# Two transformer blocks on one core: the order of the wide and the narrow matmuls in the two-half weight blocks

## The chip, the cores and the metric

The kernel runs on one core of one Trainium2 chip. The metric is the device time of one execution in microseconds (us). Three runs of the kernel before stand behind the median.

## What is computed

The reference is two blocks over 256 tokens of width 2048, all in float32. The first is a sliding-window attention with a gated short convolution beside it, an output projection and a gate. The second has a recurrent branch, an attention over the 64 best keys of each token, and a layer of 16384 small experts, of which each token takes 16 for each of 8 heads. Nearly all of the work is products of 256 tokens with 2048-wide weight matrices. The part that matters most here is the expert layer:

```
xf = rmsnorm(x, g)                       # 256 tokens x 2048
z  = xf . u[e]     for every expert e    # 16384 experts, 128 blocks of 128
act = gelu(z) * gate[e]                  # the gate is 0 for experts that a token did not pick
out = sum over e of act * v[e]
```

The kernel computes z for all experts densely. It builds the gate table from the picks with small products of one-hot rows, one for each token ("gate products").

## The kernel before, in words

**Units and slots.** All weights come as one stream of 904 units of 128x1024 floats (512 KB). SyncE loads them into four slots of `raw`. Each float32 weight is split in two rounded halves: ScalarE copies `raw` into `w_hi` (`split_hi`, the ACTIVATE of L470), and VectorE subtracts it from `raw` and writes `w_lo` (`split_lo`, L479). Two units make a pair, and one pair is one block of 128 output columns over all 2048 inputs. The slots hold two pairs, so that the splits work two pairs ahead of TensorE (`ahead`).

**The semaphores of a slot.** `hi_ready` counts units copied by ScalarE, `lo_ready` units subtracted by VectorE, `unit_done` units that TensorE has finished. ScalarE may write unit k of `w_hi` when unit k-4 is done: `act.wait_ge(unit_done, 2 * pair + u - 3)`. SyncE loads a slot of `raw` again when `lo_ready` says that its unit is subtracted.

**The two-half form.** `halves_out` (L510 to L528) makes one block. For each of its 16 rows of tiles it runs a wide matmul (L519: the tile of `w_hi` against 512 columns, the high and the low half of the activations side by side) and a narrow one (L526: the tile of `w_lo` against the 256 columns of the high half). It does so unit by unit: eight wide, eight narrow, eight wide, eight narrow. `unit_done` is counted behind the narrow ones of each unit. The result lies in one PSUM bank, whose second half is then copied by ScalarE (`low_half`, L532) and whose first half is added to it by VectorE (`add_halves`, L537, which counts `summed`).

**Who calls it.** 240 blocks are made so: 32 in the convolution, 32 in the recurrent branch, 32 in the heads, 32 in the router turns, 16 in the stage `u_decode`, 64 in the stage `u_gates` and 32 in the stage `u_late`. The other products have forms of their own (`tokens_out`, `columns_out`, `expert`) and are not touched.

**The stage `u_gates`**, 64 blocks, i = 0 to 31 and n = 0, 1. TensorE waits before each block until the GELU of the block two before is done, and puts four gate products (L2307) between the wide and the narrow matmuls of the second unit:

```
L2313 for n in range(2):
L2313     pe.wait_ge(gelu_ready[n], i + (2 * PH + 1))
L2314     halves_out(..., banks[2 + n], between=lambda: four_tokens(i, n))
```

ScalarE's order in one turn is written out in `gates_turn` (L1077 to L1090):

```
ahead(split_hi, act, "u_gates", i, 2, n, units=(0,))    # first unit, two pairs ahead
save_gelu(i, n - 1)                                     # GELU of the block before (L1072), its DMA (L1074)
(two copies out of the banks of the gate products, L1084)
ahead(split_hi, act, "u_gates", i, 2, n, units=(1,))    # second unit
low_half(act, GZ[:, n, :], banks[2 + n])                # L532
```

VectorE's order in one turn (L1854 to L1861) is: `split_lo` of the first unit, four `weighted` tiles for the next gate products (`four_tiles`, L1848), `split_lo` of the second unit, `add_halves`, and two additions out of the banks of the gate products (L1842). GpSimd makes the four `hot` tiles (L663).

**The stage `u_decode`** has ScalarE's order `split_hi` of the first unit, GELU of the block before (L1049) with its DMA (L1051), `low_half`, `split_hi` of the second unit; VectorE puts large pieces of the router's decoding between its splits (`next_low`). TensorE waits there for `summed` of the block two before. In the other stages, but for the recurrent branch, ScalarE splits both units of a pair one behind the other. In the first router block TensorE waits ahead of the second unit's wide matmuls for the low halves of the activations (`fills`, L513), which VectorE is then still writing (L1199).

Of the kernel before, what the change touches and what calls it, by code (L numbers as in the profile page):

```python
# [35 lines left out]
P = 128  # L36
S = 256
TT = S // P
D = 2048
KT = D // P  # L40
# [94 lines left out]
def build(nc, stream, x, p_t, rows, consts, params, rg_w, ukv, keys_t, out):  # L135
    ctx = ExitStack()
    with ctx:
        def sb(name, shape, dt=F32):
            return ctx.enter_context(nc.sbuf_tensor(name, shape, dt))
# [6 lines left out]
        w_hi = sb("w_hi", [P, SLOTS, UNIT], F32R)  # L146
        w_lo = sb("w_lo", [P, SLOTS, UNIT], F32R)
        act2 = sb("act2", [P, KT, 2, S], F32R)
        act_hi = act2[:, :, 0, :]
# [310 lines left out]
        def unit_slot(odd, u):  # L460
            return 2 * odd + u
# [48 lines left out]
        def halves_out(pe, pair, odd, bank, units=(0, 1), between=None, fills=None):  # L510

            for u in units:
                if fills and u == 1:  # L513
                    pe.wait_ge(act_lo_ready, fills * KT)
                s = unit_slot(odd, u)
                pe.wait_ge(hi_ready, 2 * pair + u + 1)
                for kk in range(8):
                    k = 8 * u + kk
                    pe.matmul(bank[:, :], w_hi[:, s, kk * P:(kk + 1) * P],  # L519
                              act2[:, k, :, :].rearrange("p a n -> p (a n)"), start=(k == 0), stop=False)  # L520
                if u and between:
                    between()
                pe.wait_ge(lo_ready, 2 * pair + u + 1)
                for kk in range(8):
                    k = 8 * u + kk
                    mm = pe.matmul(bank[:, 0:S], w_lo[:, s, kk * P:(kk + 1) * P], act_hi[:, k, :], start=False,  # L526
                                   stop=(k == KT - 1))
                mm.then_inc(unit_done, 1)  # L528

        def low_half(act, dest, bank):  # L530
# [1429 lines left out]
        def _(pe):  # L1960
# [63 lines left out]
            def conv_pair(j, n):  # L2024
                wait_summed(pe, block_of("conv", j, 4, n - 4))
                halves_out(pe, pair_of("conv", j, 4, n), n % 2, banks[n])
# [144 lines left out]
            def rnn_inputs(j):  # L2171
                wait_summed(pe, block_of("rnn", j, 2, 0 - 2))
                halves_out(pe, pair_of("rnn", j, 2, 0), 0, banks[0])

            def rnn_queries(j):
                wait_summed(pe, block_of("rnn", j, 2, 1 - 2))
                halves_out(pe, pair_of("rnn", j, 2, 1), 1, banks[1])
# [310 lines left out]
```

## Time and profile before

| | |
|---|---|
| median of three runs | 2757.71 us (2756.69 to 2760.06) |
| the profiled execution's own time | 2760.17 us |
| its span, first to last instruction | 2758.4 us |
| mean granted TensorE clock | 0.995 |
| TensorE matmul (PE), weight load (PEld) | 99%, 85% of the span busy |
| VectorE (DVE), ScalarE (ACT), GpSimd (POOL) | 69%, 50%, 13% |
| DMA | 523.16 MB, 190 GB/s |

PE is the matmul row and PEld the weight loads beside it. Matmuls are pipelined: the duration of one is longer than the time from its start to the next one's start, so a busy PE is not a PE at its peak. What is read below is therefore from start to start.

### The profile page before, as it was taken

The page shows a single profiled execution, that of the slowest core. Times are in us where ns is not written, and L with a number is a line of the kernel's source. Part 1 is how long each engine was busy: PE and PEld are TensorE (multiplying, and loading weights), DVE is VectorE, ACT ScalarE, POOL GpSimd, SP SyncE. Part 2 cuts the span into 40 slices and gives each one's busy share as a digit, 9 for nine tenths or more (in the row PEclk, how much of TensorE's full clock was granted, in tenths as well). Part 3 has the DMA queues.
Part 4 walks back from the last instruction along what each step waited for, and adds up shares of the span by engine and source line. Part 5 has one row for each costly group of instructions (what it writes and reads, how often), then busy time and mean ns, then how long its engine had stood idle before and what let it go on. Part 6 is the DMA issues. An engine that isn't in the chain of part 4 may idle for free.

```text
span 2758.4 us, 48218 instructions
## 1 busy us (share of the span) xinstructions
PE 2717.2 (99%) x14432; PEld 2338.8 (85%) x14432; DVE 1892.3 (69%) x3048; ACT 1392.6 (50%) x2117; POOL 358.0 (13%) x422
## 2 busy tenths in 40 slices
PE   8999999999999999999999999999999999999998
PEld 6888878888888888878888888888888888888887
DVE  6666665668986666479997888886665555555555
ACT  5455445556665444454546555555544444444444
POOL 0000000000000111001103666661000000000000
PEclk9999999999999999999999999999999999999999
DMA  6644455564555444555556655556666666655564
GB/s 246 190 157 158 151 168 184 187 218 161 168 181 160 152 153 151 176 198 189 189 187 207 196 193 195 194 196 207 208 214 215 219 216 215 216 191 195 192 237 159
DMA packets 162771, 523.16 MB, mean 190 GB/s; under 512 B 18080, under 2 KB 42912, under 8 KB 161696
## 3 DMA queue, kind: packets, MB, share of 16 engines
q1 hardware_dynamic: 131904, 480.44, 52.9%
q10 hardware_dynamic: 30816, 42.09, 4.3%
q8 instruction: 26, 0.43, 0.1%
q14 instruction: 25, 0.20, 0.0%
HBM read 505.68 MB, written 16.78 MB: 189 GB/s over the span
## 4 chain that ended last, share of the span: by engine, by line
PE 85%; issue 10%; DVE 3%; ACT 1%; POOL 1%; DMA 0%; POOLq 0%; DVEq 0%; ACTq 0%; SPq 0%
PE bank L519 27%; PE bank L526 14%; PE bank L2338 8%; PE bank L2340 8%; PE bank L2339 8%; PE bank L559 4%; PE bank L561 4%; PE bank L560 4%; PE bank L2307 1%; DVE w_lo L479 1%; PE bank L502 1%; PE bank L503 1%; PE bank L504 1%; POOL big L642 0%; PE bank L2167 0%
## 5 line engine op out<-in xcount | busy, mean ns | idle before, releaser
L479 DVE TENSOR_TENSOR w_lo<-raw,w_hi 128x1024 fp32r<-128x1024 f32 x904 | 1097.2, 1224 | 715.9 <-ACT w_hi L470 710.5
L470 ACT ACTIVATE w_hi<-raw 128x1024 fp32r<-128x1024 f32 x904 | 954.0, 1060 | 963.9 <-PE bank L526 370.9
L519 PE MATMUL bank<-act,w_hi 128*128 128x512 f32 x3840 | 976.2, 396 | 5.3 <-ACT big L992 3.0
L519 PEld LDWEIGHTS bank<-act,w_hi 128*128 128x128 f32 x3840 | 693.5, 189 | 136.0 <-issue 10.1
L526 PEld LDWEIGHTS bank<-act,w_lo 128*128 128x128 f32 x3840 | 520.7, 191 | 33.3
L526 PE MATMUL bank<-act,w_lo 128*128 128x256 f32 x3840 | 536.3, 282 | 0.0
L2338 PE MATMUL bank<-w_hi,expert_act 128*128 128x512 f32 x1008 | 392.3, 389 | 0.1
L2340 PE MATMUL bank<-w_hi,expert_act 128*128 128x512 f32 x1008 | 392.2, 389 | 0.0
L2339 PE MATMUL bank<-w_lo,expert_act 128*128 128x512 f32 x1008 | 392.1, 389 | 0.0
L663 POOL TENSOR_SCALAR hot<-cst,stat 128x128 fp32r<-128x128 f32 x256 | 255.1, 1011 | 129.1 <-PE bank L2307 128.7
L2338 PEld LDWEIGHTS bank<-w_hi,expert_act 128*128 128x128 f32 x1008 | 189.3, 188 | 39.6 <-DVE cst L537 0.5
L2340 PEld LDWEIGHTS bank<-w_hi,expert_act 128*128 128x128 f32 x1008 | 189.3, 188 | 39.3
L2339 PEld LDWEIGHTS bank<-w_lo,expert_act 128*128 128x128 f32 x1008 | 189.3, 188 | 39.2
L559 PE MATMUL bank<-w_hi,act 128*128 128x512 f32 x320 | 126.4, 395 | 2.2 <-DVE act L1423 0.9
L561 PE MATMUL bank<-w_hi,act 128*128 128x512 f32 x320 | 125.3, 392 | 0.0
L560 PE MATMUL bank<-w_lo,act 128*128 128x512 f32 x320 | 125.2, 391 | 0.0
L669 POOL TENSOR_TENSOR big<-big 128x1024 f32<-128x1024 f32 x2 | 5.8, 2880 | 874.9 <-DVE big L1921 874.9
L1848 DVE SCALAR_TENSOR_TENSOR weighted<-cst,slot_t 128x256 fp32r<-128x256 f32 x256 | 115.9, 510 | 0.0
L631 POOL TENSOR_TENSOR big<-big 128x256 f32<-128x256 f32 x16 | 11.2, 701 | 496.8 <-DVE big L537 496.8
L559 PEld LDWEIGHTS bank<-w_hi,act 128*128 128x128 f32 x320 | 60.6, 189 | 16.3 <-DVE act L1423 1.3
L561 PEld LDWEIGHTS bank<-w_hi,act 128*128 128x128 f32 x320 | 60.5, 189 | 12.9
L560 PEld LDWEIGHTS bank<-w_lo,act 128*128 128x128 f32 x320 | 60.7, 190 | 12.3
(315 smaller groups left out, 2524.8 us busy)
## 6 DMA issues: line engine op xcount, KB each, us to landing
raw<-in_stream SPq DMA_DIRECT2D x904, 512.0 KB, 3.4
z_kept<-cst ACTq DMA_DIRECT2D x96, 128.0 KB, 2.1
cst<-z_kept ACTq DMA_DIRECT2D x96, 128.0 KB, 3.8
big<-in_ukv ACTq DMA_DIRECT2D x16, 512.0 KB, 4.6
big<-in_x SPq DMA_DIRECT2D x2, 1024.0 KB, 9.3
big<-in_rows ACTq DMA_DIRECT2D x2, 1024.0 KB, 9.2
big<-in_rg_w ACTq DMA_DIRECT2D x1, 2048.0 KB, 11.5
x_kept<-big ACTq DMA_DIRECT2D x1, 2048.0 KB, 6.6
```

What stands on the lines that cost most here:

```text
L470: act.activation(w_hi[:, s, :], raw[:, s, :], ACT.Copy).then_inc(hi_ready, 1)
L479: dve.tensor_tensor(w_lo[:, s, :], raw[:, s, :], w_hi[:, s, :].bitcast(F32), ALU.subtract).then_inc(lo_ready, 1)
L519: pe.matmul(bank[:, :], w_hi[:, s, kk * P:(kk + 1) * P], act2[:, k, :, :].rearrange("p a n -> p (a n)"), start=(k == 0), stop=False)
L526: mm = pe.matmul(bank[:, 0:S], w_lo[:, s, kk * P:(kk + 1) * P], act_hi[:, k, :], start=False, stop=(k == KT - 1))
L559: pe.matmul(outs[t], a_hi, hi, start=(k == 0), stop=False)
L560: pe.matmul(outs[t], a_hi, lo, start=False, stop=False)
L561: mm = pe.matmul(outs[t], a_lo, hi, start=False, stop=(k == KT - 1))
L663: pool.tensor_scalar(hot[:, s % 4, :], iota, idx8[:, s:s + 1], None, ALU.is_equal)\
L1848: dve.scalar_tensor_tensor(out=weighted[:, s, :, :], in0=iota.unsqueeze(1).broadcast_to([P, 2, P]), scalar=first_index[:, bass.ds(tok, 1)] ...
L2338: pe.matmul(o, a_hi, hi, start=first, stop=False, skip_group_check=True)
L2339: pe.matmul(o, a_hi, lo, start=False, stop=False, skip_group_check=True)
L2340: mm = pe.matmul(o, a_lo, hi, start=False, stop=False, skip_group_check=True)
```

## The change

`halves_out` runs its loop over the units twice. The first loop runs the wide matmuls of both units, sixteen in all; the second runs the narrow matmuls of the first unit, then the callers' own work (`between`, the gate products) and then the narrow matmuls of the second unit. The products, their operands and their number stay as they are, and so do all counts of the semaphores: `unit_done` is still counted behind the narrow matmuls of each unit. Nothing changes on the other engines.

```
             for u in units:
                 if fills and u == 1:
                     pe.wait_ge(act_lo_ready, fills * KT)
-                s = unit_slot(odd, u)
                 pe.wait_ge(hi_ready, 2 * pair + u + 1)
                 for kk in range(8):
                     k = 8 * u + kk
-                    pe.matmul(bank[:, :], w_hi[:, s, kk * P:(kk + 1) * P],
+                    pe.matmul(bank[:, :], w_hi[:, unit_slot(odd, u), kk * P:(kk + 1) * P],
                               act2[:, k, :, :].rearrange("p a n -> p (a n)"), start=(k == 0), stop=False)
+            for u in units:
                 if u and between:
                     between()
                 pe.wait_ge(lo_ready, 2 * pair + u + 1)
                 for kk in range(8):
                     k = 8 * u + kk
-                    mm = pe.matmul(bank[:, 0:S], w_lo[:, s, kk * P:(kk + 1) * P], act_hi[:, k, :], start=False,
-                                   stop=(k == KT - 1))
+                    mm = pe.matmul(bank[:, 0:S], w_lo[:, unit_slot(odd, u), kk * P:(kk + 1) * P], act_hi[:, k, :],
+                                   start=False, stop=(k == KT - 1))
                 mm.then_inc(unit_done, 1)
```

## Rows read from the trace of the kernel before

**Rows 1.** The page, part 1: busy time, share of the span, instructions.

```profile
PE 2717.2 (99%) x14432; PEld 2338.8 (85%) x14432; DVE 1892.3 (69%) x3048; ACT 1392.6 (50%) x2117; POOL 358.0 (13%) x422
```

**Rows 2.** The timeline where PE began `u_decode`, behind ACT L992 and a new loop.

```profile
1390.52 0.60 ACT L992 ACTIVATE big<-bank 128x512 f32<-128x512 f32 x1 [0.68 <-ACT cst L1002]
...
1391.45 2.07 PE L519 MATMUL bank<-act,w_hi 128*128 128x512 f32 x4 [3.02 <-ACT big L992]
```

**Rows 3.** The waits of PE over the whole span: us in total, times, longest.

```profile
PE bank L519 <- DVE cst L537: 0.5, 3, 0.2
```

**Rows 4.** Windows: PE, PEld, DVE, ACT, POOL busy (x), PEclk, DMA share, GB/s.

```profile
660.00:720.00 60.00, 60.00 (x340) 52.70 (x339) 58.50 (x104) 38.25 (x56) 4.89 (x10) 1.00 0.54 174
...
1440.00:1500.00 60.00, 59.17 (x339) 51.38 (x338) 45.13 (x60) 40.56 (x58) 10.29 (x14) 1.00 0.66 211
1500.00:1560.00 60.00, 60.00 (x359) 53.42 (x358) 51.91 (x90) 33.32 (x59) 40.30 (x45) 1.00 0.59 193
```

**Rows 5.** The timeline of a stretch of `u_gates`: start, us, engine, line [idle before].

```profile
1498.35 2.00 PE L519 MATMUL bank<-act,w_hi 128*128 128x512 f32 x8
...
1500.19 1.12 PE L526 MATMUL bank<-act,w_lo 128*128 128x256 f32 x8
...
1501.14 2.00 PE L519 MATMUL bank<-act,w_hi 128*128 128x512 f32 x8
1501.34 1.06 ACT L470 ACTIVATE w_hi<-raw 128x1024 fp32r<-128x1024 f32 x1 [1.40 <-PE bank L526]
1502.31 0.40 ACT L1072 ACTIVATE cst<-cst 128x256 f32<-128x256 f32 x1
...
1502.98 0.64 PE L2307 MATMUL bank<-weighted,hot 128*128 128x256 f32 x4
...
1504.41 2.00 PE L519 MATMUL bank<-act,w_hi 128*128 128x512 f32 x8
...
1505.58 0.36 ACT L532 ACTIVATE cst<-bank 128x256 f32<-128x256 f32 x1
...
1507.21 2.00 PE L519 MATMUL bank<-act,w_hi 128*128 128x512 f32 x8
```

**Rows 6.** The timeline of PE in the last stage, the first and the 18th wide matmul.

```profile
2199.64 0.39 PE L2338 MATMUL bank<-w_hi,expert_act 128*128 128x512 f32 x1
...
2203.49 0.39 PE L2340 MATMUL bank<-w_hi,expert_act 128*128 128x512 f32 x1
```

**Rows 7.** The page, part 5: the wide matmuls, count, busy, mean.

```profile
L519 PE MATMUL bank<-act,w_hi 128*128 128x512 f32 x3840 | 976.2, 396 | 5.3 <-ACT big L992 3.0
```

**Rows 8.** The timeline where a block of `u_decode` had waited for VectorE.

```profile
1450.20 0.41 DVE L537 TENSOR_TENSOR cst<-cst,bank 128x256 f32<-128x256 f32 x1
...
1450.75 2.10 PE L519 MATMUL bank<-act,w_hi 128*128 128x512 f32 x8 [0.16 <-DVE cst L537]
...
1452.69 1.12 PE L526 MATMUL bank<-act,w_lo 128*128 128x256 f32 x8
```

**Rows 9.** The timeline of the last block of `u_decode` and the first gate products.

```profile
1482.66 2.00 PE L519 MATMUL bank<-act,w_hi 128*128 128x512 f32 x8
...
1483.88 0.40 ACT L1049 ACTIVATE cst<-cst 128x256 f32<-128x256 f32 x1
...
1484.32 0.35 ACTq L1051 DMA_DIRECT2D z_kept<-cst  x1
...
1485.65 0.38 ACT L532 ACTIVATE cst<-bank 128x256 f32<-128x256 f32 x1 [1.37 <-PE bank L526]
...
1488.94 1.67 DVE L1848 SCALAR_TENSOR_TENSOR weighted<-cst,slot_t 128x256 fp32r<-128x256 f32 x4
...
1490.75 0.74 PE L2307 MATMUL bank<-weighted,hot 128*128 128x256 f32 x4 [0.50 <-DVE weighted L1848]
```

**Rows 10.** The timeline at the first router block.

```profile
1200.16 4.00 DVE L1199 SCALAR_TENSOR_TENSOR act<-bank,par,act 128x256 fp32r<-128x256 f32 x10
...
1202.15 2.10 PE L519 MATMUL bank<-act,w_hi 128*128 128x512 f32 x8 [0.63 <-DVE act L1199]
```

More of the change, by code:

```diff
@@ L514, in halves_out @@
                     pe.wait_ge(act_lo_ready, fills * KT)
-                s = unit_slot(odd, u)
                 pe.wait_ge(hi_ready, 2 * pair + u + 1)
@@ L518, in halves_out @@
                     k = 8 * u + kk
-                    pe.matmul(bank[:, :], w_hi[:, s, kk * P:(kk + 1) * P],
+                    pe.matmul(bank[:, :], w_hi[:, unit_slot(odd, u), kk * P:(kk + 1) * P],
                               act2[:, k, :, :].rearrange("p a n -> p (a n)"), start=(k == 0), stop=False)
+            for u in units:
                 if u and between:
@@ L525, in halves_out @@
                     k = 8 * u + kk
-                    mm = pe.matmul(bank[:, 0:S], w_lo[:, s, kk * P:(kk + 1) * P], act_hi[:, k, :], start=False,
-                                   stop=(k == KT - 1))
+                    mm = pe.matmul(bank[:, 0:S], w_lo[:, unit_slot(odd, u), kk * P:(kk + 1) * P], act_hi[:, k, :],
+                                   start=False, stop=(k == KT - 1))
                 mm.then_inc(unit_done, 1)
```

## The prediction

> **What bounds the kernel now.** I read the page's busy shares first, then the waits of PE, then the windows, then the timeline of single blocks. PE is busy 99% of the span [rows 1]. The waits at the touched matmuls are few and single: the longest is 3.02 us, once [rows 2], and the waits for VectorE's sum come to 0.5 us in three [rows 3]. In the windows of the touched stages PE is busy 60.00 of 60 us, while DVE has 58.50 in the worst of them, 51.91 in `u_gates`, and ACT half of it [rows 4]. So PE's own sequence sets the time, and the change acts in two ways: through what that sequence costs from start to start, and through what it releases later than now, for an engine that PE soon needs again.
>
> **The saving in PE's own sequence.** In the middle of `u_gates` eight wide matmuls behind narrow ones take from 1501.14 to 1502.98, 1.84 us [rows 5]. In the last stage, where wide follows wide, 17 steps take from 2199.64 to 2203.49, 3.85 us, so eight would take 1.81 [rows 6]. The first eight after a turn from narrow to wide thus cost 0.03 us more. The other way: eight narrow behind wide take 0.95 (1500.19 to 1501.14), while four gate products and eight narrow take 1.43 (1502.98 to 1504.41), 0.12 each, which is 0.96 for eight [rows 5]. The change takes one turn of each kind out of each block: 0.03 less 0.01, 0.02 us. The 3840 wide matmuls at 16 a block make 240 blocks [rows 7], 4.8 us if all of it lies on the path. As the rows have two digits, the bounds are 0.01 and 0.03 a block.
>
> The Trainium skill ("TensorE: Matmul & The Clock Gate", Part 1, on the 56 ns gap) says that at the full clock a matmul starts N/2.4 GHz plus about 2.5 ns after the one before, whatever came before. By that rule the order would save nothing, and the sum below would be 3 us higher. The rows do not follow it: they have 0.227 us at 512 columns and 0.12 at 256, where the rule gives 0.216 and 0.109, and the first eight differ from later ones.
>
> **What is released later.** Take the start of a block as 0. Now the first unit is done at 1500.19 + 1.12 - 1498.35 = 2.96, and ACT, which has waited for it 1.40 us, begins 0.03 later to split the unit two pairs ahead (1501.34) [rows 5]. After the change sixteen wide come first, 1.84 + 1.81 = 3.65, and the eight narrow end 1.12 after that, at 4.77. The second unit is done when it was, and the gate products stay where they were, at 4.6: the second loop puts them behind the eight narrow of the first unit. (The short description has them ahead of all the narrow ones. The diff does not. For the loop below that would make no difference.) ACT's first split thus moves by 1.81 us, and everything behind it in ACT's order with it. No DMA is moved by itself; SyncE's reloads wait for VectorE's split and have two pairs of time.
>
> The split itself can bear it: there are two blocks until PE wants that unit. What stands behind it in ACT's order cannot. In `u_gates` that is the GELU of the block before (L1072), and PE's next block may not start without it (`gelu_ready`). From the unit's end to the GELU's end are 1502.31 + 0.40 - 1501.31 = 1.40 us [rows 5]. **Now** the GELU ends 2.96 + 1.40 = 4.36 after the block's start and the next block starts at 6.07 (1501.14 to 1507.21, a whole period): 1.7 us of cover. **After** it ends at 4.77 + 1.40 = 6.17, when PE has just run dry.
>
> **The new period.** PE starts after a wait 0.14 us behind the releasing instruction's end (1450.61 to 1450.75), and its first eight wide then take 1.94 instead of 1.84 (1450.75 to 1452.69) [rows 8]. So in the standing loop the first unit is done at 4.87, the GELU at 6.27, and the next block starts at 6.41, against 6.07 now: 0.34 us more. It holds for the 62 blocks from the third of the stage on: 62 x 0.34 = **21.1 us**. The bounds: without the slower restart 0.24 a block, 14.9 us; if the loop's branch adds 0.20 in every second block, 31 x 0.20 more, 27.3 us. (At the start of `u_decode`, where a new loop begins, PE needed 0.33 us from L992's end to its first matmul, not 0.14 [rows 2].) I take the middle, as the block of [rows 8] is the same instruction after the same kind of wait.
>
> What else could be late in that loop: ACT ends its turn with `low_half`, 1505.58 + 0.36 [rows 5]; two copies and a split stand before it. Moved by 1.8 it ends about 9.0 after the block's start, and the next turn begins at 6.41 + 4.9 = 11.3, so ACT waits still. DVE has 51.91 us of work in 60 [rows 4]; a period of 6.41 gives it 0.34 more room. The sum that the GELU needs is made in the turn before. None of these adds to it.
>
> **One-time costs.** In `u_decode` the GELU, its DMA and `low_half` stand between the two splits. In the last block (start 1482.66 - 2.79 = 1479.87) the first unit would be done at 1484.64, the GELU start one split later, 1485.64, and from a GELU's start to the end of its DMA issue are 0.79 us (1483.88 to 1484.67) [rows 9]. So `low_half` starts at 1486.45 instead of 1485.65, and the second split, DVE's sum and the four tiles (end 1490.61) come 0.8 later, and with them the first gate products, which already wait for these tiles (1490.75, 0.50 idle) [rows 9]: **0.8 us**. The first block of `u_gates` waits 0.7 for its GELU too, but inside of that. The same delay of 0.8 falls on DVE's chain early in `u_decode`, where DVE sets PE's pace for about nine blocks and its sum releases PE at 1450.61 [rows 8]: **0.8 us** again. In the first router block the wide matmuls of the second unit are due at 1202.15 + 1.94 = 1204.09, and the last low half is ready at 1204.16 [rows 10]; with the restart that is 0.2 + 0.1 = **0.3 us**. The bounds of the three together are 0.7 (the overlap with existing waits takes up the rest) and 2.5.
>
> **The saving that remains.** It does not count in the 64 blocks of `u_gates` (the period above has it), in nine of `u_decode`, nor in 16 of the recurrent branch, where DVE is busy 58.50 of 60 us [rows 4] and may hand it back: 151 x 0.02 = **3.0 us**. Bounds 1.5 and 5.
>
> In the other stages ACT splits both units one behind the other, and the second split is released when it was, so that work behind the pair comes some 0.1 us later. Cover: the sum that releases a block is the one of two or more blocks before, and DVE has idle time in between where it does not lag. In the recurrent branch the GELU's place is taken by `low_half`, which waits for the whole block anyway.
>
> **The sum.** 21.1 + 0.8 + 0.8 + 0.3 - 3.0 = 20.0 us on the profiled execution's own 2760.17, which gives 2780.2. That execution lies 2.5 us above the median of the three runs, so in terms of the median it is 2757.7 + 20.0 = 2777.7; I say **2778**. A measurement of this kernel can tell about 0.2%, 5.5 us, from no change.
>
> **Rivals.**
> (a) *The GELU keeps its cover*, and the change is not slower. The place is the start of each block in `u_gates`, the point from which it decides is a GELU that ends before 5.9 us of the block. It would need 0.3 us less on ACT than the rows give, or a wait that PE meets later than I read the code. For it speaks that PE is 100% busy there now; against it that ACT's split already waits for L526, 1.40 us [rows 5], so it follows each shift. The time: 240 x 0.02 = 4.8 us less, 2752.9, which is within 0.2% of now. Chance 0.10; a further 0.02 for a turn that costs more than I read, which would make it faster by over 0.2%.
> (b) *More stages fall into such a loop.* If the later first split cost 0.8 us in each of the recurrent branch's 16 turns, as it does once at the end of `u_decode`, 12.8 us come on top: 2791. For it: DVE is nearly full there [rows 4]. Against it: DVE arrives at that split late anyway, and PE needs its results two blocks on. Chance 0.05.
> (c) *The short stalls lower TensorE's clock.* The windows show 1.00 granted from 1440 to 1500 although PE idled several times for 0.15 to 0.5 us there [rows 4, 9], so I give it 0.01. The cost would be large: at the lower level four wide matmuls took 2.07 us [rows 2], where eight take 2.10 [rows 8], so sixteen would cost about 3.6 us more, over 62 blocks 220 us, some 3000 in all. The Trainium skill ("TensorE: Matmul & The Clock Gate", A second HAM failure mode) tells of such a case, a clock that oscillates between two levels because of micro-idles between groups of matmuls.
>
> **How the numbers follow.** My forecast has 0.82. Its bounds: low 2757.7 + 14.9 + 0.7 - 5 = 2768; high 2757.7 + 27.3 + 2.5 - 1.5 = 2786, and 2 us for the spread of the runs. That holds about nine tenths of my case, so 2767 to 2789 leaves out (a), (b), (c) and a little of it, about 0.2 in all. Slower by over 0.2%: 0.88; within 0.2%: 0.10; faster: 0.02.
>
> **What would show it.** Right: in `u_gates` blocks 6.4 us apart, each first wide matmul with about 0.1 us idle before it, put down to ACT L1072 (the modelled end of the last narrow matmul covers the rest of the stall), some 6 us of such waits in the list; ACT L470 followed at once by L1072; eight wide behind wide at 1.81 us; the other stages each shorter by a few tenths. Wrong: a period of 6.05 in `u_gates` (rival a), new waits for DVE L537 in the recurrent branch (rival b), a granted clock below 1 there (rival c), or blocks that do not get shorter by 0.02 outside of it.

## The result, and the profile after

The changed kernel takes **2782.19 us** in the median of 4 runs (2781.65 to 2783.57); the kernel before, in 4 runs (the three of its table and one more), 2757.20 (2755.14 to 2760.06). The ratio is 1.0087, with an interval of 1.0075 to 1.0099: slower, by 20.7 to 27.3 us. The profiled executions have a span of 2779.8 us against 2758.4.

The page, part 1 (busy time, share of the span, instructions), and three groups of its part 5 (busy, mean ns of one | idle before, and what ended most of it), after:

```profile
PE 2730.0 (98%) x14432; PEld 2344.6 (84%) x14432; DVE 1881.6 (68%) x3048; ACT 1374.7 (49%) x2117; POOL 327.6 (12%) x422
...
L470 ACT ACTIVATE w_hi<-raw 128x1024 fp32r<-128x1024 f32 x904 | 940.7, 1058 | 1030.6 <-PE bank L526 454.6
L518 PE MATMUL bank<-act,w_hi 128*128 128x512 f32 x3840 | 937.9, 396 | 15.2 <-ACT big L992 3.0
L518 PEld LDWEIGHTS bank<-act,w_hi 128*128 128x128 f32 x3840 | 707.0, 188 | 175.0 <-issue 31.5
```

Against [rows 1] the number of instructions is the same on every engine. PE's wide matmuls now stand on line 518, and the idle time ahead of them went from 5.3 [rows 7] to 15.2 us. The larger sign is in the row of the weight loads: they overlap the matmuls, so their gaps show what the modelled ends of the matmuls hide. They stood idle for 175.0 us, 31.5 of it "issue"; before, the same row had 136.0 and 10.1. ACT's splits waited 454.6 us for the last narrow matmul of a unit, where they had waited 370.9.

The windows of the touched stages, after (columns as in [rows 4]; the last two lie in `u_gates`):

```profile
660.00:720.00 60.00, 60.00 (x341) 52.84 (x340) 58.46 (x105) 37.38 (x56) 4.91 (x10) 1.00 0.53 174
1440.00:1500.00 60.00, 58.07 (x332) 50.49 (x331) 42.82 (x59) 37.89 (x55) 10.24 (x14) 1.00 0.63 200
1500.00:1560.00 60.00, 58.99 (x341) 51.13 (x340) 47.99 (x85) 29.48 (x55) 32.10 (x41) 1.00 0.56 183
1600.00:1660.00 60.00, 58.99 (x334) 50.91 (x335) 48.28 (x86) 30.95 (x58) 33.80 (x42) 1.00 0.55 180
```

The granted clock stays at 1.00. In the recurrent branch PE is still full. In `u_gates` PE has 341 matmuls in 60 us where it had 359 [rows 4], and DVE's work per 60 us falls with it, from 51.91 to 47.99: DVE is not what holds it up.

The timeline of one block of `u_gates`, after, to be read beside [rows 5]:

```profile
1599.85 3.92 PE L518 MATMUL bank<-act,w_hi 128*128 128x512 f32 x16
...
1603.60 1.12 PE L526 MATMUL bank<-act,w_lo 128*128 128x256 f32 x8
...
1604.55 0.64 PE L2307 MATMUL bank<-weighted,hot 128*128 128x256 f32 x4
1604.75 1.06 ACT L470 ACTIVATE w_hi<-raw 128x1024 fp32r<-128x1024 f32 x1 [2.48 <-PE bank L526]
...
1605.03 1.12 PE L526 MATMUL bank<-act,w_lo 128*128 128x256 f32 x8
...
1605.72 0.40 ACT L1072 ACTIVATE cst<-cst 128x256 f32<-128x256 f32 x1
...
1606.25 1.91 PEld L518 LDWEIGHTS bank<-act,w_hi 128*128 128x128 f32 x9 [0.30 <-issue]
1606.26 2.11 PE L518 MATMUL bank<-act,w_hi 128*128 128x512 f32 x8
```

The block starts at 1599.85. The first unit's last narrow matmul ends 4.87 later, at 1604.72. ACT, which had waited 2.48 us for it, splits at 1604.75, and then does the GELU, which ends at 1606.12. PE's next block starts 0.14 behind that, at 1606.26, a period of 6.41 us, where [rows 5] have 6.07. The eight narrow of the second unit start at 1605.03 and, at 0.12 each, the last is issued by 1605.99: PE has nothing else to issue in the time up to 1606.26.

A table by stage helps for all that follows. It holds, in us, the time from the start of a stage's first wide to that of its last narrow matmul in the two-half blocks (the entry of `u_gates` is the step from the last of these in `u_decode` to the first of its own).

| stage (blocks) | before | after |
|---|---|---|
| convolution (32) | 208.48 | 208.14 |
| recurrent branch (32) | 193.35 | 193.32 |
| heads (32) | 265.30 | 264.75 |
| first router stage (32) | 186.01 | 185.92 |
| `u_decode` (16) | 93.89 | 93.60 |
| entry of `u_gates` | 0.1 | 0.9 |
| `u_gates` (64) | 388.91 | 411.28 |
| stage behind it (32) | 179.13 | 179.81 |

22.4 us of the loss lie in `u_gates`: its first period went from 6.83 to 6.95, the other 62 from 6.07 to 6.41 and 6.44 in turn. Elsewhere tenths are saved and given back. The stages make up the profiled executions' 21.4 us only together with the gap ahead of the first router stage, 1.5 us shorter after, which does not follow the code (see the last section).

### The profile page after: what moved, and what is told of

Its sections match the earlier page's. It is cut to its first block, busy times and chain, and to the rows that moved or that the text cites. A ratio compares the mean times of both kernels' runs of the same rounds, so it can differ in the third digit from the quotient of the medians.

```text
span 2779.8 us, 48218 instructions
## 1 busy us (share of the span) xinstructions
PE 2730.0 (98%) x14432; PEld 2344.6 (84%) x14432; DVE 1881.6 (68%) x3048; ACT 1374.7 (49%) x2117; POOL 327.6 (12%) x422
## 4 chain that ended last, share of the span: by engine, by line
PE 85%; issue 10%; DVE 2%; ACT 1%; POOL 1%; DMA 0%; POOLq 0%; ACTq 0%; DVEq 0%; SPq 0%
PE bank L518 27%; PE bank L526 14%; PE bank L2338 8%; PE bank L2340 8%; PE bank L2339 8%; PE bank L559 5%; PE bank L561 5%; PE bank L560 5%; PE bank L2307 1%; DVE w_lo L479 1%; ACT w_hi L470 1%; PE bank L502 1%; PE bank L503 1%; PE bank L504 1%; POOL big L642 0%
## 5 line engine op out<-in xcount | busy, mean ns | idle before, releaser
L470 ACT ACTIVATE w_hi<-raw 128x1024 fp32r<-128x1024 f32 x904 | 940.7, 1058 | 1030.6 <-PE bank L526 454.6
L518 PE MATMUL bank<-act,w_hi 128*128 128x512 f32 x3840 | 937.9, 396 | 15.2 <-ACT big L992 3.0
L518 PEld LDWEIGHTS bank<-act,w_hi 128*128 128x128 f32 x3840 | 707.0, 188 | 175.0 <-issue 31.5
L526 PEld LDWEIGHTS bank<-act,w_lo 128*128 128x128 f32 x3840 | 496.9, 191 | 18.7
L526 PE MATMUL bank<-act,w_lo 128*128 128x256 f32 x3840 | 508.2, 283 | 0.0
L663 POOL TENSOR_SCALAR hot<-cst,stat 128x128 fp32r<-128x128 f32 x256 | 215.4, 858 | 185.1 <-PE bank L2307 184.8
```

What stands on the lines that cost most here:

```text
L470: act.activation(w_hi[:, s, :], raw[:, s, :], ACT.Copy).then_inc(hi_ready, 1)
L518: pe.matmul(bank[:, :], w_hi[:, unit_slot(odd, u), kk * P:(kk + 1) * P], act2[:, k, :, :].rearrange("p a n -> p (a n)"), start=(k == 0), s ...
L526: mm = pe.matmul(bank[:, 0:S], w_lo[:, unit_slot(odd, u), kk * P:(kk + 1) * P], act_hi[:, k, :], start=False, stop=(k == KT - 1))
L663: pool.tensor_scalar(hot[:, s % 4, :], iota, idx8[:, s:s + 1], None, ALU.is_equal)\
```

## The experiments

Eleven runs of ten kernels follow; each is compared with the kernel before, run beside it on the same chip.

**1. PE waits for the sum alone.** The GELU's result is needed by nobody on PE; what the next block on this bank needs is that VectorE has added the bank's content up. So, on top of the changed kernel:

```
-                    pe.wait_ge(gelu_ready[n], i + (2 * PH + 1))
+                    wait_summed(pe, block_of("u_gates", i, 2, n - 2))
                     halves_out(pe, pair_of("u_gates", i, 2, n), n, banks[2 + n], between=lambda: four_tokens(i, n))
```

> The changed kernel, but in u_gates TensorE waits before a block for the sum of the block two before (as it does in u_late) and no longer for its GELU; the bank is free once the sum is made. Theory (the GELU stands on ScalarE behind a split that is released 1.81 us later): blocks of u_gates 6.05 us apart instead of 6.42, no waits for L1072, total about 2757 - 240 x 0.02 + 1 = 2753 us. Rival 1 (the late release makes the tiles of the gate products late, or DVE or POOL set the period): the period stays at 6.4, 2782 us. Rival 2 (sixteen wide in a row cost TensorE itself more): also 2782 us.

Measured: 2758.77 us (2757.02 to 2760.68, 11 runs) against 2758.45; ratio 1.0003, 0.9994 to 1.0012. The loss is gone. The timeline of `u_gates` in this kernel:

```profile
1600.21 3.82 PE L518 MATMUL bank<-act,w_hi 128*128 128x512 f32 x16
...
1605.02 1.06 ACT L470 ACTIVATE w_hi<-raw 128x1024 fp32r<-128x1024 f32 x1 [2.02 <-PE bank L526]
...
1605.98 0.40 ACT L1072 ACTIVATE cst<-cst 128x256 f32<-128x256 f32 x1
...
1606.26 2.00 PE L518 MATMUL bank<-act,w_hi 128*128 128x512 f32 x8
```

PE starts its next block 6.05 us after the last, at 1606.26, while the GELU still runs (until 1606.38). ACT's order and the late split are the same as after; only the edge from the GELU to PE is cut, so this edge is what closed the loop. The forecast of 2753 was missed all the same: the saving of the change shows in the trace (periods of 6.05 instead of 6.07, 32 blocks of the heads 0.56 us shorter) but not in the time, because the one-time costs take it back. One of them is new, the first gate products wait 1.5 us for VectorE where they had waited 0.5:

```profile
PE bank L2307 <- DVE weighted L1848: 1.5, 1, 1.5
```

**2. The same wait in the kernel before.** The same line changed there, to see whether the wait itself has a price without the change.

> The kernel before with the same wait for the sum instead of the GELU. Theory: the GELU ends 4.36 us after a block's start and is wanted at 5.9, so the wait costs nothing there: 2757 us, within 1 us of the kernel before, period 6.07. If TensorE's sequencer loses something at that wait even so: up to 0.1 us a block, 6 us faster.

Measured: 2759.70 (2756.24 to 2761.04, 11 runs); ratio 1.0005, 0.9996 to 1.0014, and all stages as before. So the wait costs nothing where it has 1.7 us of cover, and experiment 1 is no gain of its own that hides the change's loss.

**3. The GELU ahead of the split.** Another way to cut the loop, on ACT's side, on top of the changed kernel:

```
-                    ahead(split_hi, act, "u_gates", i, 2, n, units=(0,))
                     if not (first and not n):
                         save_gelu(i, n - 1)
+                    ahead(split_hi, act, "u_gates", i, 2, n, units=(0,))
```

> The changed kernel, but in ScalarE's turn in u_gates the GELU of the block before and its DMA come ahead of the split of the first unit instead of behind it; TensorE still waits for the GELU. Theory: the sum that the GELU needs is ready some 4.5 us after a block's start, so the GELU ends by 5.0, ahead of 5.9, and the split starts at 4.9 or at most 0.5 later: period 6.05, total 2753 to 2754 us. If the wait for the GELU hurts by itself and not by ScalarE's order: 2782 us.

Measured: 2793.76 (2791.69 to 2794.53, 4 runs); ratio 1.0128, 1.0113 to 1.0144. **A miss**, and on the wrong side of the changed kernel. PE's waits and the timeline of a round in this kernel:

```profile
PE bank L518 <- ACT cst L1072: 14.0, 58, 0.3
```

```profile
1601.76 0.42 ACT L1072 ACTIVATE cst<-cst 128x256 f32<-128x256 f32 x1 [2.66 <-DVE cst L537]
1602.33 3.92 PE L518 MATMUL bank<-act,w_hi 128*128 128x512 f32 x16 [0.25 <-ACT cst L1072]
1602.34 0.34 ACTq L1074 DMA_DIRECT2D z_kept<-cst  x1
1602.81 1.06 ACT L470 ACTIVATE w_hi<-raw 128x1024 fp32r<-128x1024 f32 x1 [0.64 <-ACT cst L1072]
...
1603.99 1.23 DVE L479 TENSOR_TENSOR w_lo<-raw,w_hi 128x1024 fp32r<-128x1024 f32 x1 [1.59 <-ACT w_hi L470]
...
1605.13 1.67 DVE L1848 SCALAR_TENSOR_TENSOR weighted<-cst,slot_t 128x256 fp32r<-128x256 f32 x4
...
1606.72 1.22 DVE L479 TENSOR_TENSOR w_lo<-raw,w_hi 128x1024 fp32r<-128x1024 f32 x1
...
1607.86 0.41 DVE L537 TENSOR_TENSOR cst<-cst,bank 128x256 f32<-128x256 f32 x1
...
1608.30 0.42 ACT L1072 ACTIVATE cst<-cst 128x256 f32<-128x256 f32 x1 [2.66 <-DVE cst L537]
```

What I had left out: the GELU now waits for VectorE's sum (2.66 us), and everything behind it on ACT with it. The first split follows the GELU, its store and its issue time; DVE's low part follows the split; behind this stand, in DVE's order, the four tiles, the second low part and the sum, and this sum releases the next GELU. From GELU to GELU it is 1601.76 to 1608.30, 6.54 us, and no PE instruction is in that round. In the order of the change the split went first, and the GELU found its sum long done (1603.52 + 0.41, GELU at 1605.72). One loop was cut and a longer one closed; this is read from the timeline, no further run varied it.

**4. The change outside of `u_gates` only**, the old order kept there (a copy of the old function, called from this one stage).

> The change in the 176 blocks outside of u_gates, the old order in the 64 blocks of u_gates. Theory: 176 x 0.02 = 3.5 us saved, less 0.8 us in u_decode: about 2754.5 us, period of u_gates 6.07. Rival 3 (part of the loss sits in the other stages): above 2758 us.

Measured: 2759.89 (2757.68 to 2760.59, 11 runs); ratio 1.0004, 0.9995 to 1.0013. No loss, and no saving either that the runs can tell; 2754.5 was forecast, and the time lies above the 2758 that was named as the sign of costs in the other stages, though the kernel before, beside it, has 2758.45 itself. By stage: convolution -0.34, recurrent branch -0.06, heads -0.56, first router stage -0.09, the stage behind `u_gates` -0.47. These 1.5 us are given back in `u_decode` (+1.2) and at the entry of `u_gates` (0.9 instead of 0.1). The one-time costs of the other stages are there, as large as their saving, and the 25 us are not.

**5. The change in `u_gates` only**, the counterpart.

> The kernel before, with the change in u_gates alone; all other stages keep eight and eight. Loop theory: u_gates carries the whole loss, its blocks 6.41 us apart instead of 6.07, the stage 22.4 us longer as in the changed kernel, the other stages as before. Time 2759 + 22.4 + about 0.7 for the later entry or the next stage's start = 2782. Rival (the other stages give back or take a share of their own): if the other stages of the changed kernel saved what was forecast (3 us), this one should lie 3 us above the changed kernel, at 2785; if they cost something, below it, 2779.

Measured: 2782.64 (2779.90 to 2782.92, 4 runs); ratio 1.0087, 1.0072 to 1.0103. By stage: `u_gates` +21.94, the stage behind it +1.28, the convolution, the recurrent branch, the heads and the first router stage within 0.01 of before. The whole loss of the change is here; all its other stages together come to nothing. The 1.28 was in no forecast: it is one late block, the third of the stage behind `u_gates`, and the period ahead of it (7.24 instead of 5.96). That place in the timeline of the kernel before:

```profile
1877.37 0.42 ACT L1072 ACTIVATE cst<-cst 128x256 f32<-128x256 f32 x1 [1.35 <-DVE cst L537]
1877.82 0.35 ACTq L1074 DMA_DIRECT2D z_kept<-cst  x1
1881.44 0.36 ACTq L1102 DMA_DIRECT2D cst<-z_kept  x1
1882.01 2.01 ACT L470 ACTIVATE w_hi<-raw 128x1024 fp32r<-128x1024 f32 x2 [4.23 <-DMA z_kept<-cst]
...
1886.03 2.10 PE L519 MATMUL bank<-act,w_hi 128*128 128x512 f32 x8 [0.22 <-DVE cst L537]
```

And after the change:

```profile
1899.17 0.42 ACT L1072 ACTIVATE cst<-cst 128x256 f32<-128x256 f32 x1 [1.35 <-DVE cst L537]
1899.62 0.35 ACTq L1074 DMA_DIRECT2D z_kept<-cst  x1
...
1903.94 2.01 ACT L470 ACTIVATE w_hi<-raw 128x1024 fp32r<-128x1024 f32 x2 [4.34 <-DMA z_kept<-cst]
...
1907.95 3.91 PE L518 MATMUL bank<-act,w_hi 128*128 128x512 f32 x16 [1.54 <-DVE cst L537]
```

The stage starts at 1874.48 before and 1895.11 after. The last GELU of `u_gates` comes 2.89 us behind that before, and 4.06 after, because ACT's turn is later against PE's. Its store, the landing of the store (which the load back waits for, over 4 us of ACT's idle time), the splits and VectorE's sum hang on it in one chain, and PE's wait at the end of it grows from 0.22 to 1.54. The stall in `u_gates` is not its cause, the later release is: in experiment 1, which has no stall, that GELU comes at 4.06 and the period is 7.16. With four, six, seven and eight wide matmuls ahead (experiments 10, 7, 8 and the change) the GELU comes at 3.15, 3.62, 3.83 and 4.06, and the period is 6.31, 6.73 (6.98 in experiment 11), 6.96 and 7.27.

**6. The gate products ahead of all narrow matmuls**, as the short description of the change has it and the diff has not. The prediction said in passing that for the loop this would make no difference; working out the numbers for this run, I already had to take that back.

```
+            if between:
+                between()
             for u in units:
-                if u and between:
-                    between()
                 pe.wait_ge(lo_ready, 2 * pair + u + 1)
```

> The changed kernel, but the gate products stand ahead of all sixteen narrow matmuls, as the short description of the change has it. The theory (a loop: first unit done, split, GELU, next block) gives period = time of the first unit's end + 1.40 + 0.14. The gate products now delay that end by 0.47 us, to 5.34 in a stalled block: period 6.88 instead of 6.42, total about 2782 + 62 x 0.46 = 2811 us. My prediction said that this place makes no difference to the loop; if that was right, 2782. If the order alone and not the release cost the time: 2782 too.

Measured: 2813.53 (2812.61 to 2814.88, 4 runs); ratio 1.0199, 1.0182 to 1.0216. The waits of PE and the timeline of `u_gates` in this kernel:

```profile
PE bank L518 <- ACT cst L1072: 36.7, 62, 0.7
```

```profile
1600.68 0.64 PE L2307 MATMUL bank<-weighted,hot 128*128 128x256 f32 x4
1601.16 2.08 PE L526 MATMUL bank<-act,w_lo 128*128 128x256 f32 x16
1602.32 1.06 ACT L470 ACTIVATE w_hi<-raw 128x1024 fp32r<-128x1024 f32 x1 [2.95 <-PE bank L526]
1603.28 0.40 ACT L1072 ACTIVATE cst<-cst 128x256 f32<-128x256 f32 x1
1603.82 3.94 PE L518 MATMUL bank<-act,w_hi 128*128 128x512 f32 x16 [0.58 <-ACT cst L1072]
```

The four gate products take 0.48 us of start to start (1600.68 to 1601.16), they now stand between the wide matmuls and the first unit's narrow ones, and the loop grows by as much: the mean period is 6.91 instead of 6.42. It is the loop's formula with one more term: what delays the unit's end enters the period one for one. ACT's part of the loop was varied in no run, but it reads the same here: the last of the first unit's narrow matmuls ends at 1602.28 (1601.16, seven steps of 0.12 and a length of 0.28), the GELU 1.40 later, and PE starts 0.14 behind that.

**7 and 8. Six, and seven, of the second unit's eight wide matmuls go ahead.** A dose, to find the point at which the GELU loses its cover. The function of the change runs the first eight wide, then six (or seven) of the second unit, the first eight narrow, the two (or one) wide that are left, `between`, and the last eight narrow:

```
+            wide(0, range(8))
...
+            wide(1, range(6))
+            narrow(0)
+            wide(1, range(6, 8))
+            if between:
+                between()
+            narrow(1)
```

> The changed kernel, but only six of the second unit's eight wide matmuls stand ahead of the first unit's narrow ones, the last two behind them. First unit done at 4.32 us of a block, GELU at 5.72, wanted by 5.9: no stall, period 6.05, total 2757 to 2758 us. If the loss grew with the number of wide matmuls in a row: six eighths of it, 2775 us.

> The same with seven of the eight ahead. First unit done at 4.55 us, GELU at 5.95, just past the point at which TensorE runs dry: period 6.1 to 6.2 (with the slow restart), total 2760 to 2766 us. If proportional: seven eighths of the loss, 2779 us.

Measured: with six 2754.83 (2754.27 to 2756.15, 10 runs), ratio 0.9986, 0.9976 to 0.9995; with seven 2767.23 (2765.17 to 2769.29, 6 runs), ratio 1.0035, 1.0022 to 1.0047. The timeline of `u_gates` with six (the GELU is L1080 here, the wide matmuls L515, the narrow L522):

```profile
1598.00 3.36 PE L515 MATMUL bank<-act,w_hi 128*128 128x512 f32 x14
...
1602.35 1.06 ACT L470 ACTIVATE w_hi<-raw 128x1024 fp32r<-128x1024 f32 x1 [2.01 <-PE bank L522]
...
1603.32 0.40 ACT L1080 ACTIVATE cst<-cst 128x256 f32<-128x256 f32 x1
1604.04 3.36 PE L515 MATMUL bank<-act,w_hi 128*128 128x512 f32 x14
```

and with seven:

```profile
1600.40 3.67 PE L515 MATMUL bank<-act,w_hi 128*128 128x512 f32 x15
...
1605.07 1.06 ACT L470 ACTIVATE w_hi<-raw 128x1024 fp32r<-128x1024 f32 x1 [2.14 <-PE bank L522]
...
1606.04 0.40 ACT L1080 ACTIVATE cst<-cst 128x256 f32<-128x256 f32 x1
1606.59 1.65 PE L515 MATMUL bank<-act,w_hi 128*128 128x512 f32 x6
```

With six the GELU ends at 1603.72, 5.72 us after the block's start, and the next block starts at 6.04 of its own accord. With seven it ends at 6.04 and PE starts 0.15 behind it: a period of 6.19. With eight it is 6.41. The prediction had put the point at 5.9, and the two runs lie on either side of it. A loss in proportion to the number of wide matmuls ahead would have given 2775 and 2779 us. The runs were off their own forecasts by less: six came out 2 us below 2757, seven 1 us above 2766.

**9. Four and four.** The other direction, from the kernel before: four wide, four narrow, twice per unit, so that each block has twice the turns.

```
+                for half in range(2):
+                    for kk in range(4 * half, 4 * half + 4):
...
+                    if not half:
+                        pe.wait_ge(lo_ready, 2 * pair + u + 1)
+                    for kk in range(4 * half, 4 * half + 4):
```

> The kernel before with four wide, four narrow and so on within each unit, twice as many turns. Releases stay where they were. If a turn of each kind costs 0.02 us a block: each block 0.04 longer (two more of each), 240 x 0.04 = 10 us, 2768 us; read from single starts (the first four wide behind narrow take 0.93 instead of 0.91) only 0.02 a block, 5 us, 2763 us. If the turns cost nothing: 2758 us.

Measured: 2761.24 (2758.03 to 2764.10, 10 runs); ratio 1.0009, 0.9999 to 1.0019. The sign fits a price per turn; the size is below what the expectation had and at the edge of what the runs can tell.

**10 and 11. Four of the eight ahead, and six once more.** Six ahead had been better than the expectation by 3 us, so I asked whether that is real, and whether four has it too.

> Only four of the second unit's eight wide matmuls go ahead of the first narrow one, the other four stay behind the first eight narrow ones. If each turn from narrow to wide costs what the first five wide matmuls behind it show (233, 236, 228, 232, 231 ns instead of 227) and nothing comes back in the narrow ones, a block of the stage behind u_gates takes 2.749 for twelve wide, 0.952 for eight narrow, 0.929 for four wide and 0.955 for eight narrow, 5.585 us: as before (5.587), time 2759. If the lead of the kernel with six ahead (5.560) comes from releasing ACT at a middle point, this one has it too: 2755 to 2757. In u_gates no stall in either case, the period 6.06.

> The kernel with six of the eight ahead once more, on the same chip as the one with four, since its lead over the kernel before (ratio 0.9986) is hardly larger than its interval. If the lead is real: 2754 to 2756 where before has 2758 to 2760, and blocks of 5.56 us behind u_gates and 6.04 in it. If it was chance: within 1 us of before.

Measured: four 2756.53 (2754.70 to 2758.57, 11 runs), ratio 0.9992, 0.9983 to 1.0001; six again 2754.01 (2751.22 to 2755.60, 11 runs), ratio 0.9983, 0.9974 to 0.9992. Six ahead is faster than both kernels, twice, by 0.14 and 0.17% against the kernel before. Four ahead is within its interval of the kernel before. Where six gains is seen in the steps of a block, in ns from one matmul's start to the next one's, medians over the stage behind `u_gates`, where block follows block:

```
                   wide                        narrow                       wide              narrow                            block
before             233 236 228 232 231 227x3   113 119 120x6                as the first      as the first                      5.587 us
sixteen (change)   233 236 228 232 231 227x11  113 119 120x14                                                                   5.567
four ahead         231 236 228 233 231 227x7   113 119 120x6                233 236 228 233   117 119 117 117 118 119 121 117   5.573
six ahead          234 236 228 232 231 227x9   114 119 120x6                233 236           116 112 117 118 119 121 117 117   5.560
four and four      230 231 236 228             117 118 119 121              and so on                                           5.600
```

A turn to wide costs the first five wide 25 ns in all (1160 instead of 1135). Of that, the turn back gives 8 ns (113 and 119 instead of 240), 17 net. After two wide only, they have cost 15 ns and the eight narrow behind them take 937 ns instead of 960. So with six ahead the second turn pays 8 ns instead of costing 17, and the sum is 0.027 a block less than before. Over the 240 blocks this is 6.5 us; measured are 4.2 and 4.9. In experiment 11 the stages are shorter than before (convolution -0.83, recurrent branch -0.78, heads -0.65, first router stage -0.31, `u_gates` -1.55), but for the entry of `u_gates` (+0.4) and the stage behind it with its late block (+0.2). With four ahead a block takes 5.573 and not the 5.585 of the expectation, because the eight narrow behind four wide take 946 ns and not 955. So the steps account for four as well; an earlier release of ACT is not needed for it, since PE waits for nobody in these blocks. What in the engine makes these steps uneven no run tells.

## Why the prediction was right or wrong

**The direction and the size** came out as forecast: 2778 was given, 2782.19 is measured, inside the range. The sum had 20.0, the medians differ by 25.0, and the miss can be split by the terms, with the blocks' own steps:

**The loop of `u_gates`**, forecast 21.1, measured 22.25 (22.37 less 0.12 in its first period). The mechanism is shown by five runs: cutting the edge to PE removes it (experiment 1), it is there without the rest of the change (5), and its period moves as the formula says when a term is added (6: 6.91) or taken off (7, 8: 6.04, 6.19). Its parts are right too: the first unit done 4.87 after the start, the restart 0.14, the stalled block's slower wide matmuls. ACT needed 1.40 from the unit's end to the GELU's, 4.87 to 6.27. The term was small by a little, since every second period is 6.44 instead of 6.41; the mean of 6.424 gives 62 x 0.357 = 22.1.

**The one-time costs**, forecast 1.9, measured 2.4. First router block: its period grew from 5.69 to 6.01, 0.32 against a forecast of 0.3. The entry of `u_gates`: the last period of `u_decode`, up to the first block of `u_gates`, grew from 5.59 to 6.38 and the first one behind it by 0.12, 0.9 against 0.8. But the place was named wrong. PE waits there for the GELU and no longer than before for the tiles of the gate products:

```profile
PE bank L518 <- ACT cst L1049: 0.7, 1, 0.7
...
PE bank L2307 <- DVE weighted L1848: 0.5, 1, 0.5
```

The prediction had that wait of 0.7 "inside of" the other one; it is the one that stands, and takes the other's place. Experiment 1 takes it away, and then the gate products' wait of 1.5 us appears, as the prediction would have it. That the two waits come to about the same size is luck for this term. In `u_decode` DVE was to deliver 0.8 later: its slow run of periods of 6.0 us begins three blocks earlier, and the 14 periods from the second to the fifteenth sum to 81.13 instead of 79.99, 1.1 us more. (Before, six of them are longer than 5.59, not nine as the prediction had it; after, nine.) The stage's total hides this, because its first period was 7.02 instead of 8.43. That is no gain of the change: with this stage's code as before, in experiment 5, it was 7.13. At the start of the stage, behind 3 us of idle time, the first matmuls run at the lower of the two levels: the granted clock is 0.50 from 1391 to 1394 before, and the wide matmuls of [rows 2] start 0.43 us apart, 0.23 later. How many do varies from one execution to the next.

**What was missing from the sum**: the stage behind `u_gates`, 1.28 us (experiment 5). The step that failed is "what else could be late in that loop": it put this at nothing. It looked at the loop, where ACT waits anyway, and not at what follows it: the last GELU, its store, and the load of that store in the next stage, one chain that already had released PE late before (0.22). The late release makes it, not the stall.

**The saving**, forecast 3.0, measured 1.9: 0.34 in the convolution, 0.03 in the recurrent branch, 0.55 in the heads, 0.41 in the first router stage without its first block, and 0.60 behind `u_gates` without the late one. The 0.020 per block was right where block follows block (5.587 to 5.567). Where other work stands ahead of the block the convolution saves 0.011 and the heads 0.017. In the recurrent branch PE saves 0.23 over the first 20 blocks and then waits once for VectorE's sum, a period of 6.70 instead of 6.27, which costs 0.43; the 11 blocks behind it save 0.24, and 0.03 is left. The prediction had left half of this branch's blocks out of the saving for that reason; it was all of them. Nowhere did it become the loop of rival (b).

So 22.25 + 2.4 + 1.3 - 1.9 = 24.0. The medians differ by 25.0, and the last 1.0 is in no stage that was found. The spans of the two profiled executions differ by 21.4 only: of the 24.0, 1.4 is hidden by the start of `u_decode` and 1.5 by the gap ahead of the first router stage, neither of which follows the code.

**The rule of the 56 ns gap** (the Trainium skill, "TensorE: Matmul & The Clock Gate", Part 1) does not hold here: it goes by the columns alone and would have all five orders of the table take the same time. They differ by up to 40 ns a block, with 227 and 120 ns where it gives 216 and 109. The blocks of experiments 9 and 11 (5.600 and 5.560 us) lie on either side of the kernel before (5.587), with the same 32 matmuls in another order. **A clock that oscillates** (the Trainium skill, "TensorE: Matmul & The Clock Gate", A second HAM failure mode) was not seen: 62 stalls of 0.3 us left it at 1.00 granted from 1486 to 1900, and the 0.7 of experiment 6 from 1500 to 1920. The price of that rival was a little high as well: at the lower level wide matmuls start 0.43 us apart instead of 0.23, which is 3.2 us for sixteen and not 3.6.

**Rival (a)**, the GELU that keeps its cover, is what experiment 7 is: the point at 5.9 us decides, and at 5.72 there is no stall. **In the list of signs** two were wrong. The other stages were not all shorter: the blocks of `u_decode` behind its first and the stage behind `u_gates` (+0.7) were longer. And some 6 us of waits for L1072 were expected after, and the list has 0.2 in one.

```profile
PE bank L518 <- ACT cst L1072: 0.2, 1, 0.2
```

The stall is 0.27 us a block (1605.99 to 1606.26). The modelled end of the last narrow matmul, 1605.03 + 1.12 = 1606.15, covers 0.16 of it. The 0.11 that is left is in the 15.2 us of idle time of line 518, but the wait list has no gaps as short as that. The stall shows better in the gaps of the weight loads, "issue 31.5" against 10.1 before. The wait list shows it only where more than the cover and such a short gap is left: in experiment 6, with 0.74 a block (16 narrow from 1601.16 on at 0.12 are issued by 1603.08, and PE starts at 1603.82), it has 36.7 us in 62.

**"No difference"** for the gate products ahead of all narrow ones was wrong by 31 us. It had looked at whether they lie in ACT's part of the loop; they lie in PE's.

## What to carry to other kernels

Before reordering an engine's own stream, ask for each result that it signals how much later the signal comes, and follow it through the in-order queue of the engine that takes it until something comes back to the first. The cover is a number, and the restart belongs to it: here 1.7 us less 0.14, between the shift of 1.36 us with six ahead, which costs nothing, and the 1.59 with seven, which does (1.81 with eight). A partial move that stays inside of it can have all of the gain and none of the loss in the loop. A wait that asks for a later event than it needs (the GELU instead of the sum) costs nothing until the day that something ahead of it moves; and swapping two instructions on the waiting engine can close a longer loop than the one it opens.

## What was not expected of the hardware

The time of a run of matmuls depends on the order of wide and narrow ones in a way that is more than a cost per turn: eight narrow ones take 952 ns behind eight wide, 946 behind four and 937 behind two. The first five wide behind narrow ones take 233, 236, 228, 232 and 231 ns and the later ones 227 (with seven ahead, where the eight narrow stand behind a single wide, the first take 242, 231, 232 and 231). For one order the medians agree in all executions to about 1 ns. Which resource sets it stays open: it was not tried with other shapes, or without a weight load for each matmul.

Open as well: the gap between the heads and the first router stage is 103 us in some executions (103.1 after, 102.9 in experiment 11) and 104.5 in others (before, and in experiment 5), without a relation to the code. This makes single spans differ by more than the change's savings.
